# Attention by head pairs: the next pair's weights are split into high and low parts beside units 6, 7 and 8 instead of 5, 6 and 7

## The chip, the cores and the metric

The kernel runs on one core of a Trainium2 chip. A core has five engines that run side by side, each through its own list of instructions in a fixed order, and that wait for one another through semaphores: TensorE (PE in the profile, with its weight loads as PEld), VectorE (DVE), ScalarE (ACT), GpSimd (POOL) and SyncE (SP), which here only issues DMAs. The metric is the device time in microseconds, the median of several runs.

## The reference, cut to what matters

The program is two layers of a streaming encoder over 1024 prompt tokens and 8 streams of 16 new tokens: a gated linear recurrence, then multi-head latent attention. The change lies in the prompt part of the attention:

```python
cq = rms_norm(proj[..., :Q_LORA], q_norm_g)
q = einsum('btr,re->bte', cq, w_uq)            # 16 heads x (128 + 64 rotary)
k = einsum('bsk,khn->bshn', c, w_uk)           # keys of a head, from the latent rows
v = einsum('bsk,khv->bshv', c, w_uv)
s = (q_nope @ k.T + q_rope @ kr.T) * ATTN_SCALE
p = softmax(where(mask, s, -1e30))             # chunk-causal over 128-query blocks
o = p @ v                                      # then gated, then the output projection
```

(The reference multiplies by `w_uk` on the query's side; the kernel makes each head's keys and values instead, which is the same product.)

## The kernel before, in words

**Products in three passes.** Matrices that take part in the large products are held as two parts in a reduced-precision 32-bit format, a high part (ACT rounds, `round_high`, line 103) and a low part (DVE subtracts the high part from the raw value, `round_low`, line 108). A product is three matmuls, low by high, high by low and high by high, which stand at lines 114, 115 and 116.

**Head pairs.** `heads_programs` runs over the 16 heads in 8 pairs (0 to 7). Pair 0 and pair 7 are written out, pairs 1 to 6 are a hardware loop (`pairs`, line 1871). In a pair there are 16 units, `u` = 0 to 15: a unit is one block of 128 queries of one head. Two units form a group `G`, which has one output. The units of a pair go, for each engine, through these steps:

- `scores(u)` on PE (lines 2022 to 2045): the block's scores against all keys up to its own block. PE makes the scores of unit u+3 while it is in the iteration of unit u.
- `largest(u)` on DVE: a small MEMSET for the mask (line 2304) and a row maximum (TENSOR_REDUCE, line 2308).
- `exp(u)` on ACT (line 2179), `inverted(u)` on DVE (the reciprocal of the row sum, line 2312), a scaling on POOL (line 1959).
- `turn(u)` on PE (line 2066): transposes of the weights into a bank of PSUM. `turned(u)`: ACT rounds them into `h_pt_h`, DVE makes `h_pt_l` from them.
- `values(G)` on PE (lines 2069 to 2089): the weights times the values, as three matmuls for each block of keys. It waits for `t_out`, that is for DVE's `h_pt_l` of the group's last unit. `values(2)` stands in the iteration of unit 8 and waits for the `h_pt_l` of unit 6.
- `gated(G)` on DVE (line 2330): the output times the gate.

**Work beside the units.** The table `BESIDE` puts the projections of the pair into the iterations of its units, and from unit 9 on those of the next pair: `QA0` (the first 384 columns of the first head's queries) of the next pair stands in the iteration of unit 9, `KA0` (its keys) in that of unit 11. `proj` on PE begins `QA0` with a wait for four finished weight pieces, `KA0` with a wait for all six:

```python
            if s == ("R0" if first else "QA0"):
                pe.wait_ge(S["wl_ready"], pr * WPARTS + 4)
            if s == "KA0":
                pe.wait_ge(S["wl_ready"], pr * WPARTS + WPARTS)
```

**The splits.** A pair's weights are loaded raw at the start of the pair before it (`load_w`) and split there in six pieces, four of 384 columns (the query weights, pieces 0 to 3) and two of 512 (key and value weights, pieces 4 and 5). The table `SPLITS` says beside which unit. ACT's `split_high` (line 2117) stands ahead of the unit's `turned`, DVE's `split_low` (line 2248) behind it:

```python
SPLITS = {5: (0, 1), 6: (2, 3), 7: (4, 5)}
...
                turned(pr, u)
                if u in SPLITS and not last:
                    for i in SPLITS[u]:
                        split_low(dve, pr + 1, i)
```

Each `split_low` counts `wl_ready` up by one. Pairs 0 to 6 split for the pair behind them; pair 7 has nothing to split. The pieces are called `h_w_raw`, `h_w_h` and `h_w_l` in the profile, and the queries' input `cq_h` and `cq_l`: PE's first instruction that reads a split piece reads as `ps<-cq_h,h_w_l` on line 114.

Of the kernel before, what the change touches and what calls it, by code (L numbers as in the profile page):

```python
# [1737 lines left out]
def place_of(u):  # L1738
# [25 lines left out]

BESIDE = {0: ("KB0", 0), 1: ("QB0", 0), 2: ("KB1", 0), 3: ("QB1", 0), 4: ("QB2", 0), 6: ("QL", 0),
          9: ("QA0", 1), 10: ("QA1", 1), 11: ("KA0", 1), 12: ("KA1", 1), 13: ("QA2", 1), 14: ("R0", 1), 15: ("R1", 1)}
SPLITS = {5: (0, 1), 6: (2, 3), 7: (4, 5)}
NE = 5
KEYS_FROM = 10
VALUES_FIRST = (4,8,12,)  # L1770
# [17 lines left out]
def heads_programs(nc, k, m, kept_at):  # L1788
# [328 lines left out]
    def split_high(act, pr, i):  # L2117
        if i == 0:
            act.wait_ge(S["uq_loaded"], pr * 64 + 64)
            if not (isinstance(pr, int) and pr == 0):  # L2120

                act.wait_ge(S["proj_done"], pr * NP - 1)
        if i == 4:
            act.wait_ge(S["ukv_loaded"], pr * 32 + 32)
        round_high(nc, piece(w_h, i), piece(w_raw, i)).then_inc(S["wh_ready"], 1)

    @block.scalar
    def _(act):
# [42 lines left out]
        def exp(pr, u):  # L2171
            act.wait_ge(S["max_done"], pr * UNITS + u + 1)
            if u in (0, 1, 3):

                act.wait_ge(S["rq_out"], pr * 3 + (1, 2, 3)[min(u, 2)])
            if u >= PB:

                act.wait_ge(S["t_done"], pr * len(TSTEPS) + last_turn(u - PB))
            nc.scalar.activation(weights_of(u), scores_of(u), ACT.Exp, bias=mx[:, u % PB], accum_out=rsum[:, u % PB]).then_inc(S["exp_done"], 1)  # L2179
# [19 lines left out]
        def body(pr, first, last):  # L2199
# [16 lines left out]
            for u in range(UNITS):  # L2216
                if u % 2 == 0:
                    beside(u)
                    if u == 0:
                        exp(pr, 2)  # L2220
                if u in SPLITS and not last:
                    for i in SPLITS[u]:
                        split_high(act, pr + 1, i)
# [24 lines left out]
    def split_low(dve, pr, i):  # L2248
        dve.wait_ge(S["wh_ready"], pr * WPARTS + i + 1)
        round_low(nc, piece(w_l, i), piece(w_raw, i), piece(w_h, i)).then_inc(S["wl_ready"], 1)  # L2250

    @block.vector
    def _(dve):
# [60 lines left out]
        def turned(pr, u):  # L2314
            for i, (uu, place, w) in enumerate(TSTEPS):
                if uu != u:
                    continue
                dve.wait_ge(S["t_high"], pr * len(TSTEPS) + i + 1)
                G, half = unit(u)
                at = (slice(None), slice(place, place + w), slice(half * P, half * P + P))  # L2320
                round_low(nc, pt_l[G % 2][at], bank[:, 4 + i % TB, 0:w * P].rearrange("p (a q) -> p a q", a=w), pt_h[G % 2][at]).then_inc(S["t_out"], 1)
# [22 lines left out]
        def body(pr, first, last):  # L2344
# [15 lines left out]
            for u in range(UNITS):  # L2360
# [21 lines left out]
# [4 lines that stand above are left out]
# [1053 lines left out]
```

## Time and profile before

| | |
|---|---|
| median of three runs (lowest, highest) | 1886.08 us (1885.78, 1888.19) |
| the profiled execution's own time | 1887.08 us |
| its span, first to last instruction | 1885.3 us |
| PE busy, share of the span | 1864.6 us, 99% |
| DVE busy | 1054.3 us, 56% |
| ACT busy | 740.4 us, 39% |
| POOL busy | 434.6 us, 23% |
| head pairs, from the first `cq_h` matmul on | 931.6 us to some 1545 us of the span |

Times inside the span are microseconds from its start. In the timeline view a row gives the start, the duration, engine, line, operation, output<-inputs and shape, and in brackets the time for which the engine stood idle before it with what ended that time; several equal instructions in a row are merged (x2) and then the duration reaches from the first one's start to the last one's end. Matmuls are pipelined: each lasts longer than the distance between two starts.

### The profile page before, as it was taken

What the parts mean: (1) busy time and instruction counts of PE and PEld (TensorE: products, weight loads), DVE (VectorE), ACT (ScalarE), POOL (GpSimd) and SP (SyncE); (2) the same over time, 40 slices, a digit from 0 to 9 for tenths busy, and PEclk for the clock granted to TensorE, in tenths of its full rate; (3) what the DMA queues carried; (4) which work ended last, traced back from release to release, by engine and by line L of the source; (5) the groups of instructions that cost most, each with busy time, mean ns of one, the idle gap of its engine ahead of it and who ended that gap; (6) DMA issues with size and microseconds to landing.
All of it is one profiled execution on the core that took longest, in us unless ns stands there. A gap on an engine that the chain in (4) does not pass through costs nothing.

```text
span 1885.3 us, 30278 instructions
## 1 busy us (share of the span) xinstructions
PE 1864.6 (99%) x11256; PEld 1746.2 (93%) x11256; DVE 1054.3 (56%) x1867; ACT 740.4 (39%) x1292; POOL 434.6 (23%) x342
## 2 busy tenths in 40 slices
PE   9999999999999999999999999999999989999998
PEld 8899999999988999999999999999999989998886
DVE  3126665566768612332366667666766669953642
ACT  3233233323422222221355555555555567751100
POOL 0002233323311010000032433434324344400000
PEclk9999999999999999999999999999999999999999
DMA  7120222222155412223312111211121176563521
GB/s 261 55 87 25 83 82 83 71 82 72 59 190 172 131 46 72 82 78 116 112 29 75 42 53 48 63 50 46 50 74 39 40 219 182 181 222 129 162 90 45
DMA packets 162059, 178.91 MB, mean 95 GB/s; under 512 B 23376, under 2 KB 137424, under 8 KB 161712
## 3 DMA queue, kind: packets, MB, share of 16 engines
q1 hardware_dynamic: 155632, 158.08, 26.4%
q10 hardware_dynamic: 6160, 19.14, 2.9%
q8 instruction: 63, 1.03, 0.2%
q0 software_dynamic: 176, 0.43, 0.1%
q14 instruction: 28, 0.23, 0.0%
HBM read 130.86 MB, written 46.76 MB: 94 GB/s over the span
## 4 chain that ended last, share of the span: by engine, by line
PE 59%; DVE 4%; ACT 3%; issue 3%; DMA 1%; SPq 0%; ACTq 0%; DVEq 0%
PE ps L114 18%; PE ps L116 17%; PE ps L115 17%; PE ps L2066 2%; ACT h_p L2179 1%; DMA scratch_og<-h_gate 1%; DVE h_mx L2308 1%; PE ps L2044 1%; PE ps L2045 1%; DVE h_pt_l L108 1%; ACT h_pt_h L103 1%; PE ps L2619 1%; PE ps L1358 0%; PE ps L2723 0%; PE ps L2642 0%
## 5 line engine op out<-in xcount | busy, mean ns | idle before, releaser
L1959 POOL TENSOR_SCALAR h_p<-h_p,h_rsum 128x128 f32<-128x128 f32 (+7 forms) x128 | 219.6, 1716 | 427.7 <-DVE h_rsum L2312 427.3
L114 PE MATMUL ps<-act_h,a_w_l 128*128 128x384 f32 x576 | 204.3, 355 | 0.0
L116 PE MATMUL ps<-act_h,a_w_h 128*128 128x384 f32 x576 | 195.0, 339 | 0.0
L115 PE MATMUL ps<-act_l,a_w_h 128*128 128x384 f32 x576 | 194.9, 338 | 0.0
L114 PE MATMUL ps<-act_h,m_c_l 128*128 128x384 f32 x480 | 163.0, 340 | 0.0
L116 PE MATMUL ps<-act_h,m_c_h 128*128 128x384 f32 x480 | 162.6, 339 | 0.0
L115 PE MATMUL ps<-act_l,m_c_h 128*128 128x384 f32 x480 | 162.5, 339 | 0.0
L108 DVE TENSOR_TENSOR h_pt_l<-ps,h_pt_h 128x128 fp32r<-128x128 f32 (+2 forms) x192 | 100.5, 552 | 61.4 <-ACT h_pt_h L103 61.3
L103 ACT ACTIVATE h_pt_h<-ps 128x128 fp32r<-128x128 f32 (+2 forms) x192 | 87.1, 490 | 94.7 <-PE ps L2066 94.5
L2179 ACT ACTIVATE h_p<-ps,h_mx 128x128 f32<-128x128 f32 (+7 forms) x128 | 94.8, 741 | 66.6 <-DVE h_mx L2308 66.4
L114 PE MATMUL ps<-o_w,o_g 128*128 128x512 f32 x288 | 112.3, 390 | 0.0
L116 PE MATMUL ps<-o_w,o_g 128*128 128x512 f32 x288 | 112.1, 389 | 0.0
L115 PE MATMUL ps<-o_w,o_g 128*128 128x512 f32 x288 | 112.0, 389 | 0.0
L114 PEld LDWEIGHTS ps<-act_h,a_w_l 128*128 128x128 f32 x576 | 108.2, 188 | 4.1 <-issue 3.3
L115 PEld LDWEIGHTS ps<-act_l,a_w_h 128*128 128x128 f32 x576 | 108.3, 188 | 3.4 <-issue 3.3
L116 PEld LDWEIGHTS ps<-act_h,a_w_h 128*128 128x128 f32 x576 | 108.1, 188 | 0.0
L114 PE MATMUL ps<-cq_h,h_w_l 128*128 128x384 f32 x288 | 102.1, 355 | 0.6
L2308 DVE TENSOR_REDUCE h_mx<-ps 128x1 f32<-128x128 f32 (+7 forms) x128 | 97.0, 758 | 4.6 <-DVE ps L2304 0.3
L116 PE MATMUL ps<-cq_h,h_w_h 128*128 128x384 f32 x288 | 96.7, 336 | 0.0
L115 PE MATMUL ps<-cq_l,h_w_h 128*128 128x384 f32 x288 | 96.7, 336 | 0.0
L114 PE MATMUL ps<-h_pt_h,h_v_l 128*128 128x256 f32 x320 | 89.5, 280 | 3.5 <-DVE h_pt_l L108 1.8
L115 PE MATMUL ps<-h_pt_l,h_v_h 128*128 128x256 f32 x320 | 90.5, 283 | 0.0
(318 smaller groups left out, 4972.4 us busy)
## 6 DMA issues: line engine op xcount, KB each, us to landing
a_w_raw<-in_w_in_a SPq DMA_DIRECT2D x24, 512.0 KB, 5.2
m_c_raw<-in_w_in_b SPq DMA_DIRECT2D x20, 512.0 KB, 4.1
scratch_gate<-m_sg SPq DMA_DIRECT2D x16, 576.0 KB, 5.1
o_w_raw<-in_w_out_b SPq DMA_DIRECT2D x16, 512.0 KB, 6.0
h_gate<-scratch_gate SPq DMA_DIRECT2D x62, 128.0 KB, 2.0
scratch_og<-h_gate SPq DMA_DIRECT2D x62, 128.0 KB, 1.7
s_ct_raw<-in_cache_ckv_turned SPq DMA_DIRECT2D x7, 1024.0 KB, 5.3
o_g_raw<-scratch_og SPq DMA_DIRECT2D x24, 256.0 KB, 4.0
```

Source lines behind the costliest of these rows:

```text
L103: return nc.scalar.activation(high, x, ACT.Identity)
L108: return nc.vector.tensor_tensor(low, x, high.bitcast(F32), ALU.subtract)
L114: nc.tensor.matmul(out, ll, rh, start=first, stop=False)
L115: nc.tensor.matmul(out, lh, rl, start=False, stop=False)
L116: return nc.tensor.matmul(out, lh, rh, start=False, stop=last)
L1959: nc.gpsimd.tensor_scalar(x, x, rsum[:, u % PB], None, ALU.mult).then_inc(S["p_ready"], 1)
L2044: nc.tensor.matmul(out, rq[:, e, q], k.kr_l[:, kc], start=False, stop=False)
L2045: mm = nc.tensor.matmul(out, rq[:, e, q], k.kr_h[:, kc], start=False, stop=True)
L2066: mm = nc.tensor.transpose(bank[:, 4 + i % TB, j * P:j * P + P], p[:, u % PB, key * P:(key + 1) * P], k.ident[:])
L2179: nc.scalar.activation(weights_of(u), scores_of(u), ACT.Exp, bias=mx[:, u % PB], accum_out=rsum[:, u % PB]).then_inc(S["exp_done"], 1)
L2308: nc.vector.tensor_reduce(mx[:, u % PB], scores_of(u), AX.X if n <= BANK else AX.XY, ALU.max, negate=True).then_inc(S["max_done"], 1)
L2619: mm = nc.tensor.transpose(b[:, x * P:x * P + P], p[:, j // 2, s:s + P], k.ident[:])
```

## The change

One table is changed. Each of the three steps of two pieces goes one unit later: pieces 0 and 1 from unit 5 to unit 6, 2 and 3 from 6 to 7, 4 and 5 from 7 to 8. It counts for pairs 0 to 6. Nothing is added or taken away, and the lists of PE, POOL and SP stay as they are.

```diff
-SPLITS = {5: (0, 1), 6: (2, 3), 7: (4, 5)}
+SPLITS = {6: (0, 1), 7: (2, 3), 8: (4, 5)}
```

On DVE, in pair 0 (`h_pt_l_4717` belongs to units of odd groups, here first unit 5 and later unit 7, `h_pt_l_4716` to those of even groups, here unit 6), the list before reads, from the end of unit 5 to the end of unit 7:

```order
L108 TENSOR_TENSOR h_pt_l_4717<-ps,h_pt_h_4715 128x3x128
L108 TENSOR_TENSOR h_w_l<-h_w_raw,h_w_h 128x384 x2
L2312 RECIPROCAL h_rsum<-h_rsum 128x1
L2304 MEMSET ps 64x64
L2308 TENSOR_REDUCE h_mx<-ps 128x1
L108 TENSOR_TENSOR h_pt_l_4716<-ps,h_pt_h_4714 128x4x128
L108 TENSOR_TENSOR h_w_l<-h_w_raw,h_w_h 128x384 x2
L2312 RECIPROCAL h_rsum<-h_rsum 128x1
L2304 MEMSET ps 64x64
L2308 TENSOR_REDUCE h_mx<-ps 128x1
L108 TENSOR_TENSOR h_pt_l_4717<-ps,h_pt_h_4715 128x4x128 x2
L108 TENSOR_TENSOR h_w_l<-h_w_raw,h_w_h 128x512 x2
```

And now, at the same place:

```order
L108 TENSOR_TENSOR h_pt_l_4717<-ps,h_pt_h_4715 128x3x128
L2312 RECIPROCAL h_rsum<-h_rsum 128x1
L2304 MEMSET ps 64x64
L2308 TENSOR_REDUCE h_mx<-ps 128x1
L108 TENSOR_TENSOR h_pt_l_4716<-ps,h_pt_h_4714 128x4x128
L108 TENSOR_TENSOR h_w_l<-h_w_raw,h_w_h 128x384 x2
L2312 RECIPROCAL h_rsum<-h_rsum 128x1
L2304 MEMSET ps 64x64
L2308 TENSOR_REDUCE h_mx<-ps 128x1
L108 TENSOR_TENSOR h_pt_l_4717<-ps,h_pt_h_4715 128x4x128 x2
L108 TENSOR_TENSOR h_w_l<-h_w_raw,h_w_h 128x384 x2
```

The second pair of 384-column pieces (2 and 3), with which the fourth piece is finished, stood ahead of unit 7's two `h_pt_l` and now stands behind them; the first pair went from ahead of unit 6's `h_pt_l` to behind it.

On ACT, in pair 0, from unit 6 to unit 8, the list before reads (the line 2179 rows are the exponentials of units 9 and 10):

```order
L103 ACTIVATE h_w_h<-h_w_raw 128x384 x2
L103 ACTIVATE h_pt_h_4714<-ps 128x4x128
L2179 ACTIVATE h_p,h_rsum<-ps,h_mx 128x640
L103 ACTIVATE h_w_h<-h_w_raw 128x512 x2
L2179 ACTIVATE h_p,h_rsum<-ps,h_mx 128x256
L103 ACTIVATE h_pt_h_4715<-ps 128x4x128 x2
L103 ACTIVATE h_pt_h_4714<-ps 128x128
```

And now:

```order
L103 ACTIVATE h_w_h<-h_w_raw 128x384 x2
L103 ACTIVATE h_pt_h_4714<-ps 128x4x128
L2179 ACTIVATE h_p,h_rsum<-ps,h_mx 128x640
L103 ACTIVATE h_w_h<-h_w_raw 128x384 x2
L2179 ACTIVATE h_p,h_rsum<-ps,h_mx 128x256
L103 ACTIVATE h_pt_h_4715<-ps 128x4x128 x2
L103 ACTIVATE h_w_h<-h_w_raw 128x512 x2
L103 ACTIVATE h_pt_h_4714<-ps 128x128
```

Ahead of unit 6's `h_pt_h` there is a pair of 384 columns as before, though now the first one; between the exponentials of units 9 and 10 stands a pair of 384 columns in place of one of 512, and the 512-column pair stands ahead of unit 8's `h_pt_h`.

## Rows read from the trace of the kernel before

**Rows 1.** The page: the span and three engines, busy us (share) x instructions.

```profile
span 1885.3 us, 30278 instructions
PE 1864.6 (99%) x11256; PEld 1746.2 (93%) x11256; DVE 1054.3 (56%) x1867; ACT 740.4 (39%) x1292; POOL 434.6 (23%) x342
```

**Rows 2.** Waits of PE, whole span: us in total, times, longest us.

```profile
PE ps L2066 <- DVE h_pt_l L108: 3.6, 1, 3.6
PE ps L114 <- DVE h_pt_l L108: 1.8, 7, 0.4
PE ps L114 <- PEq L83: 1.2, 1, 1.2
```

**Rows 3.** Timeline of PE in pair 3, units 6 to 9.

```profile
1207.52 0.31 PE L2045 MATMUL ps<-kr_h,h_rq 128*128 128x320 f32 x1
...
1208.69 1.04 PE L2066 MATMUL ps<-ident,h_p 128*128 128x128 f32 x8
1209.97 0.38 PE L114 MATMUL ps<-h_pt_h,h_v_l 128*128 128x256 f32 x1 [0.24 <-DVE h_pt_l L108]
...
1213.22 0.27 PE L2066 MATMUL ps<-ident,h_p 128*128 128x128 f32 x1
1213.25 0.42 PE L114 MATMUL ps<-cq_h,h_w_l 128*128 128x384 f32 x1
```

**Rows 4.** Timeline of DVE in pair 3, units 5 to 7.

```profile
1206.11 1.16 DVE L108 TENSOR_TENSOR h_pt_l<-ps,h_pt_h 128x512 fp32r<-128x512 f32 x2 [0.72 <-ACT h_pt_h L103]
1207.18 1.02 DVE L108 TENSOR_TENSOR h_w_l<-h_w_raw,h_w_h 128x384 fp32r<-128x384 f32 x2
...
1208.28 0.11 DVE L2304 MEMSET ps<- 64x64 f32 x1
1208.42 0.82 DVE L2308 TENSOR_REDUCE h_mx<-ps 128x1 f32<-128x640 f32 x1
1209.16 0.68 DVE L108 TENSOR_TENSOR h_pt_l<-ps,h_pt_h 128x512 fp32r<-128x512 f32 x1
1209.76 1.02 DVE L108 TENSOR_TENSOR h_w_l<-h_w_raw,h_w_h 128x384 fp32r<-128x384 f32 x2
...
1211.00 0.42 DVE L2308 TENSOR_REDUCE h_mx<-ps 128x1 f32<-128x256 f32 x1
1212.55 1.29 DVE L108 TENSOR_TENSOR h_pt_l<-ps,h_pt_h 128x512 fp32r<-128x512 f32 x2 [1.12 <-ACT h_pt_h L103]
1213.76 1.28 DVE L108 TENSOR_TENSOR h_w_l<-h_w_raw,h_w_h 128x512 fp32r<-128x512 f32 x2
```

**Rows 5.** Timeline of ACT in pair 3, units 6 to 8.

```profile
1208.30 0.60 ACT L103 ACTIVATE h_pt_h<-ps 128x512 fp32r<-128x512 f32 x1 [0.46 <-PE ps L2066]
...
1211.46 0.47 ACT L2179 ACTIVATE h_p<-ps,h_mx 128x256 f32<-128x256 f32 x1 [0.26 <-DVE h_mx L2308]
...
1211.93 1.08 ACT L103 ACTIVATE h_pt_h<-ps 128x512 fp32r<-128x512 f32 x2
1213.61 0.28 ACT L103 ACTIVATE h_pt_h<-ps 128x128 fp32r<-128x128 f32 x1 [0.60 <-PE ps L2066]
1215.64 0.49 ACT L2155 ACTIVATE h_qn_h<-ps 128x384 fp32r<-128x384 f32 x1 [1.75 <-PE ps L116]
```

**Rows 6.** Timeline of PE: the first query matmul in pairs 0 and 6.

```profile
986.65 0.42 PE L114 MATMUL ps<-cq_h,h_w_l 128*128 128x384 f32 x1
...
1439.50 0.42 PE L114 MATMUL ps<-cq_h,h_w_l 128*128 128x384 f32 x1
```

**Rows 7.** Timeline of DVE: the low parts of unit 7 in pairs 0 and 6.

```profile
986.02 1.29 DVE L108 TENSOR_TENSOR h_pt_l<-ps,h_pt_h 128x512 fp32r<-128x512 f32 x2 [1.12 <-ACT h_pt_h L103]
...
1438.80 1.29 DVE L108 TENSOR_TENSOR h_pt_l<-ps,h_pt_h 128x512 fp32r<-128x512 f32 x2 [1.12 <-ACT h_pt_h L103]
```

**Rows 8.** Windows: length, then busy us (x instructions) of five engines, PEclk, DMA.

```profile
557.50:560.00 2.50, 1.28 (x6) 0.79 (x5) 0.00 (x0) 0.00 (x0) 0.24 (x4) 1.00 0.02 7
1535.00:1540.00 5.00, 4.39 (x25) 4.28 (x25) 3.25 (x7) 3.93 (x8) 1.87 (x1) 0.66 1.07 360
```

## The prediction

> **What bounds the kernel now.** I read the page first [rows 1]: PE is busy for 99% of the span, DVE for 56%, ACT for 39%. So PE sets the end, and a change on DVE and ACT, which is all this one is, counts only through PE's waits. The list of PE's waits comes next [rows 2]: one kind recurs, PE waiting for an `h_pt_l` at line 114, 7 times, 0.4 us at the longest; there are seven pairs that split weights, 0 to 6. Nothing in that list names `h_w_l`: so far the split weights are always ready before PE asks.
>
> The timeline of PE in pair 3 shows where the recurring wait lies [rows 3]. The last transposes of unit 7 start at 1208.69, eight of them, 1.04 us in all, so they end at 1209.73; `values(2)` starts at 1209.97 and had to wait for an `h_pt_l`. That is the one of unit 6, which ends at 1209.16 + 0.68 = 1209.84 [rows 4]; PE goes on 0.13 later. The wait counts as 0.24 us idle. The next thing to see is PE's first query matmul of the next pair (`QA0`, unit 9): it starts at 1213.25, right behind the one transpose of unit 8 at 1213.22, with no wait. It needs pieces 0 to 3, and the fourth ended on DVE at 1209.76 + 1.02 = 1210.78 [rows 4]: 2.47 us of slack.
>
> Then the timeline of DVE [rows 4] with ACT's [rows 5] gives the order that decides everything here: unit 6's `h_pt_l`, a split, the maximum of unit 10 (to 1211.42), ACT's exponential of unit 10 (from 1211.46), ACT's `h_pt_h` of unit 7 (from 1211.93), and only then DVE's two `h_pt_l` of unit 7, 1212.55 to 1213.84, with 1.12 us of idle time before them. PE asks for piece 3 at 1213.25, in the middle of those two. The change puts pieces 2 and 3 behind them.
>
> **What the split ahead of unit 6 gave away.** Taking pieces 0 and 1 out of unit 5 (1.02 us at 1207.18) lets DVE come to unit 9's maximum sooner. That can't go before the scores of unit 9, whose last matmul ends at 1207.52 + 0.31 = 1207.83 [rows 3]; the maximum itself takes 0.82, so it ends well before 1209.24, where it ended. Now unit 6's `h_pt_h` on ACT is late: it ends at 1208.30 + 0.60 = 1208.90 and keeps that time, since it waited for PE and ACT has an equally long split ahead of it, before and after [rows 5]. So `h_pt_l` of unit 6 moves from 1209.16 to 1208.90 at the earliest: the advance is between 0 and 0.26 us. I take 0.21, leaving 0.05 for the signal (the exponential of unit 10 starts 0.04 behind the maximum that it waits for). `values(2)` then starts 0.21 sooner.
>
> **What the split behind unit 7 costs.** From unit 6's `h_pt_l` to unit 10's maximum DVE does the same instructions as before (pieces 0 and 1 have the columns of 2 and 3). ACT's exponential and `h_pt_h` follow the maximum, with a shorter split before them (384 columns for 512). So the two `h_pt_l` of unit 7 come 0.21 sooner too and end at 1213.84 - 0.21 = 1213.63. Pieces 2 and 3 follow: successive instructions overlap by 0.08 (1213.84 against the next start at 1213.76), they take 1.02, so they end at 1214.57. PE starts 0.13 later, as `values(2)` did: **1214.70 instead of 1213.25**, 1.45 us later. Worked with the advance as an open number a, it is 1.66 - a, so 1.40 to 1.66 a pair.
>
> **Does PE get it back?** I find nothing that pays. PE's order is unchanged and the 1.45 us lie in front of everything behind `QA0`. What comes next on DVE and ACT is measured against a PE that is 1.45 us later. Pieces 4 and 5 (1.28 us) now stand behind unit 8's `h_pt_l` on DVE; they must be there for `KA0` in unit 11, two projections behind `QA0`, and the queries' own low part waits for ACT's `h_qn_h` anyway, which PE's new wait moves from 1215.64 to some 1217.1 [rows 5]. On ACT the 512-column pair goes ahead of unit 8's `h_pt_h`, where there were 0.60 us of idle time; at the 1.28 us that DVE takes for such a pair [rows 4] some 0.7 would be left over, and it falls before that `h_qn_h`, for which ACT had waited 1.75. If that cover were gone, PE would pay the same 0.7 a pair. SP loads the next raw weights only at the start of the next pair, long after. POOL is released by reciprocals that come at the same time or sooner. The remaining waits of PE, such as the 3.6 us in rows 2, lie in pair 7 or outside the pairs, where nothing is split.
>
> **The sum.** In pair 0 the two `h_pt_l` of unit 7 start at 986.02 and `QA0` at 986.65, 0.63 later; in pair 6 it is 1438.80 and 1439.50, 0.70 later, as in pair 3 [rows 6, 7]. So pair 0 pays 0.07 more: 1.52 + 6 x 1.45 = **10.2 us**, and by the bounds 9.9 to 11.7. The profiled execution would go from 1887.08 (span 1885.3) to 1897.3 (span 1895.5). It lies 1.00 above the median of 1886.08; the median should go to **1896.3 us**, 0.54% slower.
>
> **The clock, where trace and rule are weighed.** Seven new idle times of about 1.4 us raise the question whether TensorE keeps its upper level, 2.4 GHz. The trace has one of nearly this length: in the window at 557.50 PE was idle for 1.22 us and the granted clock stood at 1.00 [rows 2, 8]. Behind the wait of 3.6 us in pair 7 it fell: in the window at 1535.00 the mean is 0.66, so part of those 5 us ran at 1.2 GHz. The new wait is nearest to the first, so I charge nothing. The Trainium skill, "TensorE: Matmul & The Clock Gate", section "A second HAM failure mode: psum-queue depth-cycling", says that a kernel whose matmul groups are parted often by short idle times can swing between the two levels again and again. By that rule all seven waits would be followed by a drop; the rows here don't bear it out so far, and its price is the second rival's.
>
> **The rivals.** (1) *The wait never shows: not slower.* DVE stands idle for 1.12 us ahead of unit 7's `h_pt_l` [rows 4]; if the whole chain before them came forward, piece 3 could be done before PE asks, and only the gain at `values(2)` would be left: 7 x 0.21 = 1.5 us, 1884.6. It decides at 1213.25 - 0.21 - 0.13 = 1212.91: piece 3 would have to be ready there, 1.66 sooner than I reckon. Against it: the idle time lies ahead of the `h_pt_l`, the split behind them, and DVE takes its list in order; the chain in front hangs on ACT's `h_pt_h` of unit 6, which can't move. 5%. (2) *Each wait drops the clock.* In the window at 1535.00 a mean of 0.66 over 5 us is a loss of 0.34 x 5 = 1.7 us; seven of them are 11.9, so 1886.08 + 10.2 + 11.9 = 1908.2. For it: the wait recurs every 75 us ((1439.50 - 986.65) / 6 [rows 6]) and is longer than the 1.22 that left the clock alone. Against it: one such wait stands between long dense stretches. 4%. (3) *DVE catches up by the whole pair that it no longer does in unit 5*, 1.02 us instead of 0.21: 1.66 - 1.02 = 0.64 a pair, 7 x 0.64 = 4.5, 1890.6. Against it: the same `h_pt_h` of unit 6. 5%. (4) *The change doesn't do what it says*, or PE doesn't ask for the fourth piece at `QA0`: 1886.1. The lists show that pieces 2 and 3 stand behind unit 7 and the wait for four pieces stands in the code. 2%.
>
> **How the numbers follow.** The forecast has 84%. Its own range is 9.9 to 11.7 over the median, 1896.0 to 1897.8. The spread of single runs (1885.78 to 1888.19) adds -0.3 and +2.1, and the short signal times that I read off single rows (0.04, 0.13) may be off by a quarter of a microsecond a pair, 1.7 in seven, which I set on the low side, since every cover that I missed shortens the wait: 1894.0 to 1899.9. The rivals, 16% together, lie outside. A measurement of this kernel can tell about 0.2%, 3.8 us, from no change. Slower by more than that are the forecast, the clock and the half-hidden case: 84 + 4 + 5 = 93%. Within 0.2% are rivals 1 and 4: 7%, of which I leave 1% to a gain that no step here would explain.
>
> **What the profile after should show.** In PE's waits a new row: PE at line 114 waiting for DVE's `h_w_l`, 7 times, about 1.4 us each (1214.70 less the end of the transpose, 1213.22 - 0.21 + 0.27 = 1213.28), about 10 us in all; the old `h_pt_l` row of 7 falls from 1.8 to near nothing. `QA0` starts 0.13 behind the second 384-column `h_w_l` of unit 7, and that starts where the second `h_pt_l` ends. From pair to pair the start of `QA0` should lie about 1.4 us further apart than before. The granted clock stays at 1.00 in the pairs. The forecast is wrong if `h_w_l` is no releaser of PE, if the wait is under 1 us, if PE's other waits shrink by as much, or if the clock falls behind the waits.

## The result and the profile after

The changed kernel takes 1896.38 us (median of 5 runs, 1895.65 to 1899.16) against 1886.08 (5 runs, 1885.78 to 1888.19): a ratio of 1.0049, 95% interval 1.0038 to 1.0059, so 7.2 to 11.1 us slower (the middle of the ratio is 9.2 us, the two medians lie 10.3 apart). The forecast was 1896.3, 10.2 us slower.

The page of the change, span and engines (answers to [rows 1]):

```profile
span 1894.0 us, 30278 instructions
PE 1866.5 (99%) x11256; PEld 1746.7 (92%) x11256; DVE 1054.0 (56%) x1867; ACT 739.1 (39%) x1292; POOL 435.4 (23%) x342
PEclk9999999999999999999999999999999999999999
```

The number of instructions is the same, DVE's busy time is the same within 0.3 us and ACT's within 1.3, and the span is 8.7 us longer. PE still reads 99%: the share of busy time hides a stall of half a percent. The list of PE's waits shows it (columns as in [rows 2]: us in total, times, longest):

```profile
PE ps L114 <- DVE h_w_l L108: 9.9, 7, 1.4
PE ps L2066 <- DVE h_pt_l L108: 2.2, 1, 2.2
```

A new releaser stands at its head, `h_w_l`, seven times 1.4 us; the recurring `h_pt_l` wait of line 114 (1.8 us, 7 times) is gone. Where it sits is shown by PE's timeline in pair 3 (answers to [rows 3]) and by its first query matmul in pair 6 (answers to [rows 6]):

```profile
1213.18 1.03 PE L2066 MATMUL ps<-ident,h_p 128*128 128x128 f32 x8
1214.24 0.38 PE L114 MATMUL ps<-h_pt_h,h_v_l 128*128 128x256 f32 x1
...
1217.49 0.27 PE L2066 MATMUL ps<-ident,h_p 128*128 128x128 f32 x1
1219.17 0.43 PE L114 MATMUL ps<-cq_h,h_w_l 128*128 128x384 f32 x1 [1.41 <-DVE h_w_l L108]
...
1449.67 0.43 PE L114 MATMUL ps<-cq_h,h_w_l 128*128 128x384 f32 x1 [1.41 <-DVE h_w_l L108]
```

`values(2)`, at 1214.24, is no longer held up. `QA0` stood right behind the transpose of unit 8 and now stands 1.68 us behind it. DVE's timeline in pair 3 (answers to [rows 4]) has the reason:

```profile
1213.42 0.69 DVE L108 TENSOR_TENSOR h_pt_l<-ps,h_pt_h 128x512 fp32r<-128x512 f32 x1
1214.03 1.01 DVE L108 TENSOR_TENSOR h_w_l<-h_w_raw,h_w_h 128x384 fp32r<-128x384 f32 x2
...
1215.27 0.42 DVE L2308 TENSOR_REDUCE h_mx<-ps 128x1 f32<-128x256 f32 x1
1216.82 1.29 DVE L108 TENSOR_TENSOR h_pt_l<-ps,h_pt_h 128x512 fp32r<-128x512 f32 x2 [1.12 <-ACT h_pt_h L103]
1218.02 1.02 DVE L108 TENSOR_TENSOR h_w_l<-h_w_raw,h_w_h 128x384 fp32r<-128x384 f32 x2
```

Unit 7's two `h_pt_l` end at 1218.11, pieces 2 and 3 at 1219.04, and PE starts 0.13 later. The 1.12 us for which DVE waits for ACT lie in front of the `h_pt_l`, unused; the two low parts that PE is waiting for stand behind them.

### The profile page after: what moved, and what is told of

Read it like the earlier page. It is cut to its first block, busy times and chain, and to the rows that moved or that the text cites. A ratio compares the mean times of both kernels' runs of the same rounds, so it can differ in the third digit from the quotient of the medians.

```text
span 1894.0 us, 30278 instructions
## 1 busy us (share of the span) xinstructions
PE 1866.5 (99%) x11256; PEld 1746.7 (92%) x11256; DVE 1054.0 (56%) x1867; ACT 739.1 (39%) x1292; POOL 435.4 (23%) x342
## 4 chain that ended last, share of the span: by engine, by line
PE 62%; DVE 3%; ACT 2%; issue 2%; DMA 1%; SPq 0%; DVEq 0%; ACTq 0%
PE ps L114 18%; PE ps L115 18%; PE ps L116 18%; PE ps L2066 2%; PE ps L2045 1%; PE ps L2044 1%; DMA scratch_og<-h_gate 1%; ACT h_p L2179 1%; DVE h_w_l L108 1%; ACT h_pt_h L103 1%; PE ps L2619 1%; DVE h_mx L2308 0%; PE ps L1358 0%; PE ps L2723 0%; DVE h_pt_l L108 0%
```

## The experiments

My theory: the whole cost is PE's wait at `QA0` for the fourth piece, which the change puts behind unit 7's `h_pt_l` on DVE. The rivals: the 512-column pair at unit 8 costs; each moved part has a share; the order on DVE isn't the cause, but the clock or what stands behind the later low parts. Differences are of medians to the kernel before, run beside each kernel (1887.99, 1887.93 and 1887.21 us in the three groups: it is 1 to 2 us slower there than the 1886.08 above). Each edit is shown either against the kernel before or against the change, as said ahead of it; `...` marks lines left out.

| run | kernel, us | difference, us | ratio, 95% interval |
|---|---|---|---|
| pieces 4 and 5 alone moved | 1888.08 | +0.1 | 1.0000 (0.9991 to 1.0009) |
| pieces 0 and 1 kept at unit 5 | 1894.49 | +6.5 | 1.0035 (1.0022 to 1.0049) |
| low parts ahead in unit 7 | 1885.39 | -2.6 | 0.9989 (0.9980 to 0.9998) |
| `QA0` waits piece by piece | 1886.64 | -1.4 | 0.9993 (0.9984 to 1.0002) |
| two pieces' pairs one unit later still | 1914.37 | +26.4 | 1.0138 (1.0121 to 1.0154) |
| unchanged, once more | 1887.18 | -0.8 | 0.9997 (0.9987 to 1.0007) |
| the change, once more | 1896.27 | +9.1 | 1.0048 (1.0030 to 1.0066) |

### Pieces 4 and 5 alone

The edit, against the kernel before:

```diff
-SPLITS = {5: (0, 1), 6: (2, 3), 7: (4, 5)}
+SPLITS = {5: (0, 1), 6: (2, 3), 8: (4, 5)}
```

> Only the two 512-column pieces move, from unit 7 to unit 8; pieces 0 to 3 stay beside units 5 and 6. My theory (the cost is PE's wait at QA0 for the fourth piece, which the change puts behind unit 7's low parts on DVE): piece 3 is ready at about 1210.8 in the times of the profile before, 2.4 us ahead of QA0, so no wait for h_w_l in PE's waits, the recurring h_pt_l wait of 0.24 us stays 7 times, and the time is that of the kernel before, within 1 us. Rival A (the 512-column pair at unit 8 costs, on ACT ahead of unit 8's h_pt_h and on DVE ahead of the queries' low part): 0.7 us a pair, +5 us. Rival B (every part of the move carries a share of the 10.3 us): +3 to +4 us.

Measured: no difference (by the interval 1.7 us either way, so the 5 us of rival A and the 3 to 4 of rival B are out), and PE's waits in the pairs are those of before:

```profile
PE ps L2066 <- DVE h_pt_l L108: 3.1, 1, 3.1
PE ps L114 <- DVE h_pt_l L108: 1.8, 7, 0.4
```

Within that interval the last third of the change is free. The 512-column pair at unit 8 is covered, as in the change itself, where ACT's timeline in pair 3 reads (answers to [rows 5]):

```profile
1217.15 1.16 ACT L103 ACTIVATE h_w_h<-h_w_raw 128x512 fp32r<-128x512 f32 x2
1218.19 0.28 ACT L103 ACTIVATE h_pt_h<-ps 128x128 fp32r<-128x128 f32 x1
1221.55 0.49 ACT L2155 ACTIVATE h_qn_h<-ps 128x384 fp32r<-128x384 f32 x1 [3.08 <-PE ps L116]
```

Unit 8's `h_pt_h` follows the pair at once, and then ACT has 3.08 us to spare before it gets the queries.

### Pieces 0 and 1 kept at unit 5

The edit, against the kernel before:

```diff
-SPLITS = {5: (0, 1), 6: (2, 3), 7: (4, 5)}
+SPLITS = {5: (0, 1), 7: (2, 3), 8: (4, 5)}
```

> Pieces 0 and 1 stay beside unit 5, pieces 2 and 3 go to unit 7, 4 and 5 to unit 8. Theory: QA0 waits again, since piece 3 stands behind unit 7's two h_pt_l. DVE has no split between unit 6's h_pt_l and unit 10's maximum, so the chain to unit 7's h_pt_l is some 0.45 us sooner than before (ACT's 384-column pair and its exponential of unit 10 then set it), QA0 starts about 1.2 us later than before, and values(2) keeps its 0.24 us wait: h_w_l 7 times 1.2 us in PE's waits, h_pt_l 7 times 0.24, the time 8.5 us over the kernel before (7 to 10), thus 1 to 3 us under the change. Rival B (each part has a share, pieces 0 and 1 among them): about +6.5 us. Rival C (it is the move of pieces 0 and 1 that costs): within 2 us of the kernel before.

Measured: 6.5 us, ratio 1.0035. That is under the 7 to 10 expected and just rival B's number; the interval, 4.2 to 9.3 us, holds the 8.5 too, so the time doesn't decide between the two. The waits do:

```profile
PE ps L114 <- DVE h_w_l L108: 6.5, 7, 0.9
PE ps L2066 <- DVE h_pt_l L108: 2.5, 1, 2.5
PE ps L114 <- DVE h_pt_l L108: 1.8, 7, 0.4
```

`h_w_l` is the only new wait. I had expected 1.2 us of it a pair and there are 0.93. The 1.2 was by how much `QA0` starts later, not for how long PE counts as idle: unit 8's transpose lasts to 0.24 past the place where `QA0` used to start [rows 3]. The delay itself is as expected. `QA0` of pair 6 starts at 1447.88, the first query matmul of the pairs at 931.92; before it was 1439.50 and 931.63. That is 8.38 - 0.29 = 8.09 us in seven pairs, 1.16 each. Part of what the time lacks to that is the wait in pair 7, 2.5 us here for 3.6 and 3.2 in two profiles of the kernel before (more on it below).

### Low parts ahead of unit 7's turned weights

The edit, against the change:

```diff
+                if u == 7 and not last:
+                    for i in SPLITS[u]:
+                        split_low(dve, pr + 1, i)
                 turned(pr, u)
-                if u in SPLITS and not last:
+                if u in SPLITS and u != 7 and not last:
```

> The change as it is, but in the iteration of unit 7 DVE makes the low parts of pieces 2 and 3 ahead of unit 7's two h_pt_l instead of behind them; ACT's order is that of the change. Theory: DVE stood idle for 1.12 us ahead of those h_pt_l, and the two low parts take 1.02, so unit 7's h_pt_l stay where they are and piece 3 is ready at about 1212.2 in the times of before, 0.8 us ahead of QA0: no wait for h_w_l, the whole 10.3 us gone, and the 0.2 us a pair that values(2) gains by the move of pieces 0 and 1 left over: 7 x 0.21 = 1.5 us under the kernel before (0 to -2.5). Rival A (the 512-column pair at unit 8 costs): +3 to +5 us. Rival D (the clock or something else than the order on DVE makes the cost): +8 us or more.

Measured: 2.6 us under the kernel before, 0.4 to 3.8 by the interval, which holds the 1.5 expected. With all three pairs of pieces where the change has them on ACT, and pieces 0, 1, 4 and 5 where it has them on DVE, this one exchange takes the whole cost away. DVE's timeline in pair 3:

```profile
1210.06 0.42 DVE L2308 TENSOR_REDUCE h_mx<-ps 128x1 f32<-128x256 f32 x1
1210.40 1.38 DVE L108 TENSOR_TENSOR h_w_l<-h_w_raw,h_w_h 128x384 fp32r<-128x384 f32 x2
1211.70 1.28 DVE L108 TENSOR_TENSOR h_pt_l<-ps,h_pt_h 128x512 fp32r<-128x512 f32 x2
```

And PE's, at the same place:

```profile
1212.28 0.27 PE L2066 MATMUL ps<-ident,h_p 128*128 128x128 f32 x1
1212.31 0.42 PE L114 MATMUL ps<-cq_h,h_w_l 128*128 128x384 f32 x1
```

The idle time ahead of the `h_pt_l` is filled, the fourth piece ends at 1211.78 and `QA0` is back 0.03 behind the transpose. It is the one version whose whole interval lies under the kernel before.

### `QA0` waits piece by piece

The edit, against the change (line 2066 becomes 2068 by it):

```diff
-            if s == ("R0" if first else "QA0"):
+            if s == "R0" and first:
                 pe.wait_ge(S["wl_ready"], pr * WPARTS + 4)
...
                 for a in range(4):
+                    if s == "QA0" and not first:
+                        pe.wait_ge(S["wl_ready"], pr * WPARTS + a + 1)
```

> The change as it is on ACT and DVE; on PE, QA0 of pairs 1 to 7 no longer waits for four pieces at its start but, ahead of the three matmuls of each of its four accumulation steps, for that step's own piece. Theory: pieces 0 and 1 are long ready, the third is ready at 1214.1 and the fourth at 1214.6 in the times of before, and QA0 comes to its third step at 1214.1 and to its fourth at 1214.8: it waits 0.1 to 0.3 us a pair in place of 1.4, and against the 0.2 that values(2) gains the time is that of the kernel before, -1.5 to +1 us. If the cost were the later low parts as such (Rival A: what stands behind them on DVE is late), nothing on DVE has changed and the time stays 8 to 10 us over the kernel before.

Measured: 1.4 us under the kernel before, by the interval 3.0 under to 0.4 over. ACT and DVE are untouched here; only what PE asks for at the start of `QA0` has changed. DVE's timeline in pair 3 has the low parts as late as in the change:

```profile
1211.80 1.29 DVE L108 TENSOR_TENSOR h_pt_l<-ps,h_pt_h 128x512 fp32r<-128x512 f32 x2 [1.12 <-ACT h_pt_h L103]
1213.01 1.02 DVE L108 TENSOR_TENSOR h_w_l<-h_w_raw,h_w_h 128x384 fp32r<-128x384 f32 x2
```

PE's timeline there, the transpose, the first matmul of `QA0` and the first of its third and fourth steps:

```profile
1212.47 0.27 PE L2068 MATMUL ps<-ident,h_p 128*128 128x128 f32 x1
1212.50 0.42 PE L114 MATMUL ps<-cq_h,h_w_l 128*128 128x384 f32 x1
...
1213.65 0.40 PE L114 MATMUL ps<-cq_h,h_w_l 128*128 128x384 f32 x1
...
1214.25 0.34 PE L114 MATMUL ps<-cq_h,h_w_l 128*128 128x384 f32 x1
```

The fourth step starts 0.22 after the pieces end at 1214.03, and `h_w_l` is in no wait of PE at all; I had expected 0.1 to 0.3 us a pair. So, within the interval, the late low parts cost nothing by themselves; that PE asked for all four before it used the first did.

### Pieces 2 to 5 one unit later still

The edit, against the kernel before:

```diff
-SPLITS = {5: (0, 1), 6: (2, 3), 7: (4, 5)}
+SPLITS = {6: (0, 1), 8: (2, 3), 9: (4, 5)}
```

> A larger dose of the suspected cost: pieces 0 and 1 beside unit 6, 2 and 3 beside unit 8, 4 and 5 beside unit 9. Theory (PE waits for the fourth piece and for nothing else): the two low parts now stand behind the gate product, unit 11's maximum and unit 8's h_pt_l on DVE; in the times of the profile before they end at about 1216.3, so QA0 starts at about 1216.4, 3.15 us later than before, with some 3.1 us of idle time: h_w_l 7 times 3.1 in PE's waits, and 7 x 3.15 + 0.1 = 22 us over the kernel before (20 to 24), if the clock holds. The clock's rival: with 1.4 us of idle time a pair the granted clock stayed at 1.00, but behind the wait of 2.2 to 3.6 us in pair 7 it fell in each profile; if it falls behind each of the seven waits too, 1.7 us a pair come on top: 34 us over the kernel before, and windows behind QA0 with a mean clock well under 1.00.

Measured: 26.4 us, by the interval 22.8 to 29.1: between the two numbers, 22 and 34. The waits are the theory's:

```profile
PE ps L114 <- DVE h_w_l L108: 21.8, 7, 3.1
```

The rest is for the most part the clock, but not behind each wait. Windows behind the waits of pairs 0, 1 and 6 (the granted clock is the third number from the end):

```profile
990.00:995.00 5.00, 5.00 (x22) 5.00 (x23) 0.56 (x1) 1.25 (x3) 0.00 (x0) 0.67 0.45 144
1070.00:1075.00 5.00, 5.00 (x35) 5.00 (x36) 1.39 (x4) 2.79 (x6) 1.02 (x1) 1.00 0.57 149
1460.00:1465.00 5.00, 2.23 (x11) 2.23 (x12) 2.60 (x8) 0.16 (x1) 0.92 (x1) 0.93 0.30 91
1465.00:1470.00 5.00, 5.00 (x31) 5.00 (x29) 1.39 (x4) 3.06 (x7) 2.20 (x1) 0.73 0.21 79
```

In this execution it fell in pairs 0 and 6; behind the waits of the other five pairs the 5 us read 1.00. PE did 22 matmuls in the 5 us behind pair 0's wait and 35 behind pair 1's. The lost clock is 0.33 x 5 = 1.65 us and (0.07 + 0.27) x 5 = 1.7 us; with the 22 us of the waits that makes 25.4. The span of this execution is 24.9 longer than that of the kernel before (1910.2 for 1885.3). The other three executions took 2.3 to 2.9 us longer than this one; how often the clock fell in them no trace shows.

### Both kernels once more

The kernel before and the change, each without an edit.

> The kernel before once more, for a second profile of it. The wait in pair 7 (PE at line 2066 for an h_pt_l) was 3.6 us in the profile before and 2.2 in that of the change, though nothing is split in pair 7. If that wait only varies from execution to execution with the DMAs of the gates, it differs from 3.6 here too (2 to 4), and the span with it; the recurring wait for h_pt_l is 0.24 us, 7 times, as before, and no h_w_l is in the list. If it is the change that shortens it, it is 3.6 again, within 0.1. The time is that of the kernel before, within 1 us.

> The change once more, for a second profile and on another chip or at another time. Theory: QA0's wait is the same in every execution, since only engines and no DMA take part: h_w_l 7 times 1.4 us, 9.9 us in all, and the time 9 to 11 us over the kernel before. Open is the wait in pair 7 (PE at line 2066 for an h_pt_l): it was 2.2 to 2.5 us in the three profiles with a wait at QA0 and 3.1 to 3.6 in the five without. If it varies freely with the gates' DMAs, it can lie anywhere from 2 to 4 here; if PE's delay in the pairs shortens it, it is 2.2 to 2.5 again.

PE's waits of the kernel before in its second profile:

```profile
PE ps L2066 <- DVE h_pt_l L108: 3.2, 1, 3.2
PE ps L114 <- DVE h_pt_l L108: 1.8, 7, 0.4
```

And of the change in its second profile:

```profile
PE ps L114 <- DVE h_w_l L108: 9.9, 7, 1.4
PE ps L2066 <- DVE h_pt_l L108: 2.7, 1, 2.7
```

What belongs to the change comes out the same to the tenth. The wait in pair 7 differs between executions of one kernel, 3.6 and 3.2 before, 2.2 and 2.7 after. But the three kernels with a wait at `QA0` had 2.2 to 2.7 in four profiles and the four without had 3.1 to 3.6 in five, means of 2.5 and 3.4: the two groups don't overlap, so a shorter wait goes with the delay; that the delay makes it shorter is not shown. What ends it is a DMA, by DVE's timelines before and after:

```profile
1533.67 0.42 DVE L2330 TENSOR_TENSOR h_gate<-ps,h_gate 128x256 f32<-128x256 f32 x1 [3.27 <-DMA h_gate<-scratch_gate]
1542.47 0.42 DVE L2330 TENSOR_TENSOR h_gate<-ps,h_gate 128x256 f32<-128x256 f32 x1 [1.91 <-DMA h_gate<-scratch_gate]
```

The `h_pt_l` that PE waits for stands behind this gate product. By SP's timeline the load was issued 2.2 us earlier, at 1531.44 and at 1540.25, right after a wait for the store of an earlier gate to land. PE's wait begins at 1531.27 and at 1541.43, so the load comes 0.2 behind that in the one and 1.2 ahead of it in the other. What makes it come sooner stays open.

## Why the prediction was right

- **The advance from unit 5.** Taken as 0.21, bounded by 0 and 0.26. From the start of unit 7's transposes to `values(2)` it was 1209.97 - 1208.69 = 1.28 before [rows 3] and is 1214.24 - 1213.18 = 1.06 in the change: 0.22. ACT's `h_pt_h` of unit 6 was named as what holds the advance; in the change DVE's unit 9 maximum ends at 1213.37, ACT's row says that this `h_pt_h` ends at 1213.39, and the `h_pt_l` starts at 1213.42:

```profile
1212.79 0.60 ACT L103 ACTIVATE h_pt_h<-ps 128x512 fp32r<-128x512 f32 x1 [0.47 <-PE ps L2066]
```

  That PE gains some 0.2 a pair by it is what the run with the low parts ahead is left with: from its first query matmul (931.75) to `QA0` of pair 6 (1437.94) it takes 506.19 us, the kernel before 507.87, so 1.68 less over seven pairs, 0.24 each.
- **The cost behind unit 7.** Forecast: `QA0` 1.45 us later a pair (1.52 in pair 0), 10.2 in all. Measured from the first query matmul (931.98) to `QA0` of pair 6: 517.69 less 507.87, 9.82 us, 1.40 a pair. Pair 0 paid 1.42: the 0.07 put on top for it did not show. In pair 3 each link of the chain held: the split begins 0.09 before the second `h_pt_l` ends, takes 1.02, and PE follows 0.13 later. PE's idle time was forecast at 1.42 and is 1.41 to 1.42.
- **What was costed at nothing.** ACT's longer pair at unit 8 and DVE's behind it were said to be covered: 0.1 us when they move alone. POOL and SP appear in no new wait of PE.
- **What PE got back.** Forecast: nothing, since PE's other waits lie in pair 7, where nothing is split. Here the prediction was a little off: the 9.82 us stay in the pairs, but the wait in pair 7 was 2.2 for 3.6, and 0.9 us shorter in the mean of the delayed kernels. The profile's span grew by 8.7, which is the 9.82, plus 0.35 by which the pairs began later, less those 1.4, within 0.1.
- **The total, and luck.** That 1896.38 lies so close to 1896.3 is partly luck. The change took 1896.4 and 1896.3 us, but the forecast was added to 1886.08, and the kernel before was 1 to 2 us slower in the later groups; run beside it, the change was 9.1 us slower the second time. The intervals (7.2 to 11.1 and 5.7 to 12.5) hold both the 10.2 and a delay with some 0.9 paid back.
- **The clock.** Charged with nothing, and rightly: the windows over the change's waits in pairs 0 and 3, and the 5 us behind `QA0`'s start in pair 3, read 1.00; so do the 5 us behind the other six:

```profile
985.00:990.00 5.00, 3.58 (x21) 3.28 (x21) 3.84 (x11) 2.74 (x7) 2.46 (x2) 1.00 0.07 23
1214.00:1220.00 6.00, 4.56 (x30) 4.06 (x29) 4.80 (x14) 3.86 (x11) 2.58 (x2) 1.00 0.00 0
1219.17:1224.17 5.00, 5.00 (x34) 5.00 (x35) 4.12 (x10) 1.68 (x4) 1.77 (x2) 1.00 0.39 111
```

  The Trainium skill's rule ("TensorE: Matmul & The Clock Gate", "A second HAM failure mode: psum-queue depth-cycling"), by which short idle times that come often make the clock swing, is not borne out for waits of 1.4 us that recur every 77 us; no run here had waits that recur more often. With 3.1 us a wait the level did fall, behind two of seven.
- **The rivals.** That the wait never shows was named with the place that would decide it, DVE's 1.12 us ahead of the `h_pt_l`. It became true only when the split was put into that place, and then the time was the rival's: it gave 1.5 us under the kernel before, the run 0.4 to 3.8 under. Rival 3, that DVE catches up by the whole 1.02 us, failed at the `h_pt_h` of unit 6, as was held against it: the advance is 0.22.

## What to carry to other kernels

Before work is moved on an engine that is half idle, find who waits for its product and at which point of its own list: DVE worked through its list in order, and its idle time in front of an instruction was of no use to what stood behind it. Compare the time at which the product is asked for with the end of the last instruction that the move puts ahead of it; here two rows, the end of unit 7's low parts and the start of `QA0`, gave PE's delay of 9.82 us within half a microsecond. If a late product can't be helped, wait for each part where it is used: here that cost nothing that could be measured, and one wait for all four cost 9 to 10 us.

## What the runs showed of the hardware that I had not expected

The fall of TensorE's clock is not fixed by the length of a wait. In the run with two pieces' pairs one unit later still, seven waits of 3.1 us, alike to 0.01, were followed by a fall from 2.4 to 1.2 GHz in two cases (mean granted clock 0.66 over the 5 us behind pair 0's and behind pair 6's, 1.00 behind the other five; single microseconds in the falls read 0.50). Waits of 0.9 to 1.4 us, seven in each of three profiles (the change twice, and pieces 0 and 1 kept at unit 5), were followed by none. In pair 7 a wait of 2.2 to 3.6 us was followed by a fall in all nine profiles. The shortest of them, 2.2 us, is that of the change: the window from 1540.00 to 1550.00 has a mean of 0.83.

```profile
1540.00:1550.00 10.00, 7.18 (x48) 6.86 (x48) 5.99 (x12) 7.42 (x17) 6.31 (x3) 0.83 0.86 289
```

A second idle time of PE, 1.1 us for a gate (L2330), ends 3.5 us before that wait begins (1537.90 and 1541.43 in the change). So a shorter wait was followed by a fall each time where a longer one mostly was not; whether the second idle time is the reason no run here separates.
